# Query projection as three rounded products for 12 of 16 row groups, all query tiles ahead of the cross-attention output, half of its weights loaded behind them

## What is computed

```python
h = rmsnorm(x); q, k, v, u = split(h @ w_in)
x = x + concat([sliding_window_attention(q, k, v), multiscale_pool(u)]) @ w_out
x = x + memory_cross_attention(rmsnorm(x), rmsnorm(mem))   # 4 heads of 128, 256 memory tokens
x = x + hierarchical_moe(rmsnorm(x))                       # 32 experts, top 2 of one group
# memory_cross_attention(h, mem_n):
q = rmsnorm((h @ xq_w).reshape(B, S, 4, 128))              # (512x2048) @ (2048x512)
p = softmax(q . k / sqrt(128)); return (p @ v) @ xo_w      # (512x512) @ (512x2048)
```

## Time and profile before

| | us |
|---|---|
| median of 3 runs | 1630.94 (1630.66 to 1634.11) |
| the profiled execution, its own time | 1631.62 |
| its span in the profile | 1629.7 |
| PE busy | 1517.8 (93%) |
| DVE / ACT / POOL busy | 604.6 / 365.5 / 443.8 |
| HBM read | 466.99 MB, 289 GB/s over the span |

### The profile page before, as it was taken

The page is one execution under the profiler, slowest core; times in us unless marked ns, Lnnn a source line. Parts: engine busy times, 40 slices in busy tenths (PEclk is TensorE's granted clock), DMA queues, the critical chain, the costliest instruction groups (busy, mean ns, idle before and its releaser), DMA issues.

```text
span 1629.7 us, 22070 instructions
## 1 busy us (share of the span) xinstructions
PE 1517.8 (93%) x6992; PEld 848.6 (52%) x6992; DVE 604.6 (37%) x746; ACT 365.5 (22%) x702; POOL 443.8 (27%) x2170
## 2 busy tenths in 40 slices
PE   7999999999999999899899899889999889989998
PEld 7787777758887466633243333323433333333333
DVE  6755656662324433523133223313313313312324
ACT  6422334352222244421011110110011101011011
POOL 4470035420000000044243332422423324233220
PEclk9999999999999999999999999999999999999999
DMA  8332222262324111599999999999999999999997
GB/s 311 104 104 77 78 78 75 84 193 96 103 78 147 59 54 50 233 369 428 427 427 429 427 429 428 429 429 427 429 428 428 430 428 429 428 428 430 428 424 298
DMA packets 88849, 471.93 MB, mean 290 GB/s; under 512 B 4642, under 2 KB 42716, under 8 KB 62556
## 3 DMA queue, kind: packets, MB, share of 16 engines
q1 hardware_dynamic: 88232, 470.84, 71.1%
q0 software_dynamic: 464, 0.35, 0.4%
q10 hardware_dynamic: 100, 0.03, 0.0%
HBM read 466.99 MB, written 4.21 MB: 289 GB/s over the span
## 4 chain that ended last, share of the span: by engine, by line
PE 70%; DMA 18%; DVE 6%; ACT 2%; issue 2%; SPq 1%; POOL 1%; ACTq 0%; DVEq 0%
PE ps L2310 22%; DMA weight_ring<-in_expert_w_up_dram 17%; PE ps L2010 11%; PE ps L1884 10%; PE ps L2340 7%; PE ps L2267 6%; PE ps L2063 3%; DVE residual L1692 2%; PE ps L1846 1%; PE ps L2404 1%; DMA residual<-in_x_dram 1%; PE ps L2126 1%; ACT weight_ring L922 1%; PE ps L1939 1%; PE ps L2123 1%
## 5 line engine op out<-in xcount | busy, mean ns | idle before, releaser
L2310 PE MATMUL ps<-weight_ring,proj_buffer 128*64 128x512 f32 x2040 | 474.3, 605 | 41.0 <-DMA weight_ring<-in_expert_w_up_dram 39.6
L722 POOL COPY proj_buffer<-transposed_acts (+1 forms) x1968 | 300.0, 215 | 616.7 <-ACT proj_buffer L1104 480.1
L2310 PEld LDWEIGHTS ps<-weight_ring,proj_buffer 128*64 128x64 f32 x2040 | 159.1, 139 | 344.5 <-issue 282.3
L1692 DVE TENSOR_TENSOR residual<-ps,residual 128x1024 f32<-128x1024 f32 x128 | 150.8, 1220 | 248.8 <-PE ps L2267 248.2
L2340 PE MATMUL ps<-weight_ring,proj_buffer 128*64 128x512 f32 x944 | 209.2, 595 | 15.6 <-issue 13.6
L1708 DVE SCALAR_TENSOR_TENSOR y_low<-ps,proj_buffer,y_high 64x1024 fp32r<-64x1024 f32 x60 | 77.0, 1283 | 231.4 <-ACT y_high L1115 230.4
L2340 PEld LDWEIGHTS ps<-weight_ring,proj_buffer 128*64 128x64 f32 x944 | 71.2, 137 | 136.1 <-issue 133.6
L1115 ACT ACTIVATE y_high<-ps,proj_buffer 64x1024 fp32r<-64x1024 f32 x60 | 66.5, 1109 | 285.0 <-PE ps L2340 284.3
L1884 PE MATMUL ps<-mix_high,w_in_high 128*128 128x512 f32 x288 | 117.3, 407 | 1.4 <-issue 1.4
L1104 ACT ACTIVATE proj_buffer<-ps 128x512 f32<-128x512 f32 x32 | 19.1, 598 | 438.0 <-PE ps L2310 438.0
L1884 PE MATMUL ps<-mix_high,w_in_low 128*128 128x512 f32 x288 | 112.3, 390 | 0.0
(11 more groups left out here) (330 smaller groups left out, 1812.7 us busy)
## 6 DMA issues: line engine op xcount, KB each, us to landing
weight_ring<-in_expert_w_down_dram SPq DMA_DIRECT2D x62, 2048.0 KB, 15.1
weight_ring<-in_expert_w_up_dram SPq DMA_DIRECT2D x61, 2048.0 KB, 20.3
weight_ring<-in_expert_w_gate_dram SPq DMA_DIRECT2D x60, 2048.0 KB, 15.9
weight_ring<-in_w_in_dram SPq DMA_DIRECT2D x18, 1024.0 KB, 5.6
weight_ring<-in_w_out_dram SPq DMA_DIRECT2D x16, 1024.0 KB, 5.0
weight_ring<-in_xkv_w_dram SPq DMA_DIRECT2D x8, 1024.0 KB, 7.5
residual<-in_x_dram SPq DMA_DIRECT2D x8, 1024.0 KB, 12.6
weight_ring<-in_expert_w_gate_dram SPq DMA_DIRECT2D x7, 1024.0 KB, 10.6
```

The costliest lines, as they stand in the source:

```text
L722: ins = g.tensor_copy(slots[:, :, j], H[:, :, ds(where[j], 1)].rearrange("p k n -> p (k n)"))
L1692: v.tensor_tensor(part, ps[:, bank:bank + 2, :].rearrange("p b n -> p (b n)"), part, ALU.add).then_inc(signal, 1)
L2310: ins = mm(ps[side * SLOTS:(side + 1) * SLOTS, 0, :], xsT[:, k, par * SLOTS:(par + 1) * SLOTS], gate_up_weights(e, u, kk), start=(k == 0), ...
```

## The change

`KQ = 12`: the first 12 of the 16 row groups of a query tile are made from rounded parts, three products each, and the last 4 as plain fp32 as before. For that

- ACT makes `xq_hi` (16 scaled copies of 128x512, the gain of the norm now multiplied into the weights) and DVE makes `xq_lo` (12), in between the steps for n = 3; the parts for k = 7 to 11 can only be written after the last output product (`halves_used`);
- the transposed rows are copied out of PSUM by ACT (`query_rows`, 4 copies a tile, no gain) in place of DVE (`turned`), and DVE subtracts (`query_rows_low`, 3 a tile). For tiles 2 and 3 ACT does so after `query_squares(0)`;
- xq_hi takes slots 8 to 11, so xo_w's parts 2 and 3 are loaded only once all queries are done, and `xo_high(2)`, `xo_high(3)`, `xo_low(2)`, `xo_low(3)` move behind `values_high(1)` and `values_out(1)`;
- PE runs `queries(3)` ahead of `cross_out(0)`.

```diff
@@ SP
             sp.wait_ge(halves_used, HALVES_IN + 32)
             for n in range(4):
+                if n == 2:
+                    sp.wait_ge(xq_done, NT)
                 sp.dma_start(xo_raw[n], xo_v[:, :, n * 512:(n + 1) * 512]).then_inc(landed[4 + 2 * n], 16)
             for u in (1, 2, 0, 3, 4, 5):
-                if u == 1:
-                    sp.wait_ge(used, SEQ_XQ + 2)
-                if u == 2:
-                    sp.wait_ge(xq_done, NT)
@@ ACT
-            for t in range(NT):
-                square_of(3, t)
-                root_of(6 + t)
+            def xq_high(first, last):
+                for k in range(first, last):
+                    if k % 4 == 0:
+                        chunk_landed(act, SEQ_XQ + k // 4)
+                    if k == 7:
+                        act.wait_ge(halves_used, HALVES_IN + 32)
+                    raw = chunk(SEQ_XQ + k // 4, XW)[:, k % 4, :]
+                    a.activation(xq_hi[k] if k < KQ else raw, raw, ACT.Copy,
+                                 scale=gT[:, G_XAT + k:G_XAT + k + 1]).then_inc(xq_hi_ready, 1)
+            def query_rows(t):
+                for b in range(4):
+                    act.wait_ge(h_turned, (6 + t) * 4 + b + 1)
+                    dst = (mix_hi if b < 3 else H)[:, 4 * b:4 * b + 4, t * P:(t + 1) * P]
+                    a.activation(dst, ps[:, b, :].rearrange("p (k n) -> p k n", n=P), ACT.Copy).then_inc(hT_ready, 1)
+            square_of(3, 0)
+            root_of(6)
+            xq_high(0, 4)
+            square_of(3, 1)
+            root_of(7)
+            xq_high(4, 7)
+            square_of(3, 2)
+            query_rows(0)
+            root_of(8)
+            xq_high(7, KQ)
+            square_of(3, 3)
+            query_rows(1)
+            root_of(9)
+            xq_high(KQ, KD)
@@ DVE
             add_part(3, 0)
             scale_rows(0)
+            xq_low(0, 4)
             add_part(3, 1)
             scale_rows(1)
+            xq_low(4, 7)
             add_part(3, 2)
-            turned(6, H, 0, G_XAT)
+            query_rows_low(0)
             scale_rows(2)
             add_part(3, 3)
-            turned(7, H, P, G_XAT)
+            xq_low(7, KQ)
+            query_rows_low(1)
             scale_rows(3)
-            turned(8, H, 2 * P, G_XAT)
-            turned(9, H, 3 * P, G_XAT)
+            query_rows_low(2)
+            query_rows_low(3)
@@ PE, turn_scaled
                     pe.wait_ge(hT_ready, T * 4 + (b - 3))
+                    if t > 0 and b < 3:
+                        pe.wait_ge(rows_lo_ready, 3 * t + b - 2)
@@ PE, queries
+                        if k < KQ:
+                            for n, (h_, w_) in enumerate(((mix_hi[:, k, part], xq_hi[k]), (mix_hi[:, k, part], xq_lo[:, k, :]),
+                                                          (rows_lo[t][:, k, :], xq_hi[k]))):
+                                ins = mm(ps[:, 4 + t % 2, :], h_, w_, start=(k == 0 and n == 0), stop=False)
+                        else:
+                            ins = mm(ps[:, 4 + t % 2, :], H[:, k, part], w[:, kk, :], start=False, stop=(k == KD - 1))
@@ PE
             xscores(1)
-            cross_out(0)
+            queries(3)
             xturn(1)
...
             xscores(2)
-            queries(3)
+            cross_out(0)
             xturn(2)
```

76 lines of the change are left out of this document (58 added, 18 removed).

## The result

The changed kernel took **1638.12 us**, median of six runs (1636.91 to 1640.53), beside 1632.34 for the kernel before in six: ratio 1.0035, 95% interval 1.0024 to 1.0046. So it is slower by 0.2 to 0.4%, 3.8 to 5.8 us; the forecast was +3.9. The 16 runs together have a median of 1637.5, and that is the figure the experiments are set against.

What follows compares the result with a forecast made beforehand. PE was taken as the path up to the first expert block, expert weight transfers after it. Terms gave +1.3 without the clock, +2.6 for the clock, +3.9 in all: 1634.8 us from a median of 1630.94, range 1629.5 to 1639.5.

Steps and rivals of the forecast that it cites:

- products: Query tiles on PE: three rounded products replace an fp32 one in 12 row groups, over four tiles -8.5 us.
- tile 3 into the banks: At turn_scaled(3): PE waits for banks that ACT and DVE empty later than before, +1.5 us (0.5 to 2.5).
- xvalues(1): Tile 1's value products: ACT does query_squares(3) before the copy they need; a wait of 2.0 us, +1.3.
- cross_out(0), third quarter: Waits for add_cross(0), behind late weight transfers and xnorm(2) on DVE: +3.7 us; 0 if transfers land early, 5.5 if slowed.
- cross_out(1), third quarter: Waits for its addition because ACT makes the router's rows ahead of xexps(3): +4.2 us (2 to 5).
- turn_queries(3): The old wait for query_scaled(3), now done some 10 us ahead, goes: -1.6 us.
- clock: Falls behind both third-quarter waits, +3.4 us, less 0.8 for the old fall at 637 that might go: +2.6 (0 to 5).
- The new work of ACT and DVE ahead of queries(0): Scaled copies and subtractions for the rounded parts, taken as covered: 0, up to +2 us if either slips.
- The drain: Rival: two table loads on the path each bring a drain, +2.8 us on top, 1637.6 us; chance 0.02.
- a rival, with 1.7: More falls and a late transfer: clock also falls at xvalues(1), +1.7, or PE is held up, +2; 1637 to 1640; 0.12.
- the clock holds: Rival: the clock holds or falls where it costs nothing; +1.3 alone, 1632 to 1633 us, no change; chance 0.27.
- the covered waits: Rival: add_cross is not late at either third quarter, so 7.9 us of waits go: -6.6, 1624.3 us; chance 0.09.

Runs made afterwards that it cites:

- The 16 runs: The changed kernel as it is, in two measurements: six runs, 1638.12 us, and ten runs, 1636.96 us.
- experiment 6: Changed kernel with dummy products on PE inside its three long waits, the waits for other engines left in place: 1633.55 us, ratio 1.0001.
- experiment 4: Kernel before with only the changed kernel's order on PE, ACT and DVE, query products plain, cross weights staged in one go: 1644.05 us, ratio 1.0062.
- experiment 3: Changed kernel with tile 1's probability copy ahead of query tile 3's squares on ACT: 1637.75 us, ratio 1.0029.
- experiment 1: Changed kernel with tile 3's exponentials ahead of token tile 0's root and scaled rows on ACT, DVE's order moved to match: 1628.81 us, ratio 0.9972.
- experiment 2: Changed kernel with the first cross output's additions on DVE taken one by one, ahead of tile 2's probabilities: 1630.99 us, ratio 0.9991.
- experiment 7: Changed kernel with 24 in place of 18 dummy products ahead of the first expert block: 1639.27 us, ratio 1.0036.
- experiment 9: Changed kernel with experiment 1 and experiment 2 together, without the moves of the probability copy and row copies: 1623.71 us, ratio 0.9945.
- the kernel with all mends: Changed kernel with experiment 1, experiment 2, experiment 3 and tile 2's row copies ahead of tile 0's squares on ACT: 1620.95 and 1620.74 us.

## Why the prediction was right, and where its steps were off

The forecast was +3.9 us and 1634.8; measured were +5.8 and +3.8, and 1638.1 and 1637.0, inside the range. Slower by over 0.2% was the likeliest case, and it came, by the waits that the prediction named. That the second difference meets the forecast within 0.1 is luck: the two measurements are 2.0 apart, and the query stage grew by 5.7 where the steps gave 1.3 + 3.4 = 4.7. The times lie 3.3 and 2.2 us over the 1634.8, of which 1.4 and 2.2 are the kernel before, which came out at 1632.3 and 1633.2 in the larger sets and not at 1630.9. By its own steps:

| step | forecast | shown |
|---|---|---|
| products | -8.5 | -8.2 (tile: 13.74 to 11.69) |
| tile 3 into the banks | +1.5 | +1.46 (1.11, then 2.26 for 1.91) |
| xvalues(1) | +1.3 | +1.30 (2.01 for 0.71) |
| xvalues(2) | +0.7 | +0.71 |
| cross_out(0), third quarter | +3.7 | +3.54 where no fall came ahead of it (+3.13 and +2.63 behind one) |
| cross_out(1), third quarter | +4.2 | +4.49 |
| turn_queries(3) | -1.6 | -1.63 |
| sum without the clock | +1.3 | +1.7; the stage of experiment 6, without a fall, is +1.8 |
| clock | +2.6 | +3.9 in the stage; the old fall stayed in one trace, and went (-1.4) in the other |

**The products and the front.** The new work of ACT and DVE ahead of queries(0) was covered: PE has no wait at turn_scaled(1) nor in queries(0), and goes from one to the next as before. Experiment 4 puts products and banks together at 7.0.

**cross_out(0), third quarter**, is right in mechanism and size wherever the clock does not fall ahead of it. I started the chain at the end of queries(3) and let the fourth part of xo_w land 7.73 us after the issue, then one high part, one low part and the softmax chain, 16.5 in all. In experiment 3 the issue stands at

```profile
584.18 0.92 SPq L524 DMA_DIRECT2D weight_ring<-in_xo_w_dram  x2
```

and ACT, which waits for the landing, starts on the fourth part at 591.87 (its rows there), 7.69 us later. In experiment 1 the issue is at 587.02, ACT starts at 594.78, also out of a wait for the landing, and the third quarter at 603.50: 7.76 and 16.48. In the changed kernel itself another path came last: the fall at xvalues(1), which I had not put into the forecast, made `values_high(1)` late, the landings were there when ACT came to them, and both low parts, 3.43 us, stood between the high parts and xmax(2). That the wait is then 3.13, and 2.63 with a shorter fall, the steps do not give. My lower bound of 0 for early landings was wrong: in experiment 4 nothing lands late and the wait is 3.19, since both low parts still stand ahead of xmax(2).

**cross_out(1), third quarter** was right in mechanism and near in size, 4.49 for 4.2. Missing from its sum is the table load ahead of root_of(10) (613.37): from the start of `values_high(2)` to the rows it takes 2.33 us where I had 2.0. The load ahead of root_of(11), which experiment 1 takes away, is no cost of the change. The kernel before has it too (at 634.33, 1.28 us), with the same wait of 1.97 behind it.

**The drain.** The two loads that came onto the path are there, and again without a drain behind them; ahead of root 3:

```profile
584.77 1.28 ACT L1066 ACT_TABLE_LOAD   x1
586.06 0.30 ACT L1066 ACTIVATE query_stats<-query_stats,eps 128x4 f32<-128x4 f32 x1
```

The root starts 0.01 us after the load's end. The drain of about 1.38 us that ScalarE: Activation LUTs of the Trainium skill, section What ACT_TABLE_LOAD costs, adds to a load would have made the waits at xvalues(1) and at cross_out(1) 1.4 longer each; they are within 0.3 of what the load alone gives. That rival is out.

**The clock** is the term that was mis-sized. I took 1.7 for each of the two waits of 4 us; they cost 1.3 and 1.4 in the first trace, so 2.7 for 3.4, though behind 5.11 and 4.49 us of idle time experiments 3 and 2 show 2.2 and 2.5. I took no fall behind the 2.0 us at xvalues(1) into the forecast (it was in a rival, with 1.7); it fell there in both traces of the changed kernel and cost 1.2 net, and held in experiments 1, 2 and 4 behind the same wait. And I booked 0.8 for a fall at 637 that might go; it stayed in the first trace and went in the second. Experiment 6 settles the size: 3.4 us by the medians and 3.9 in the stage hang on the three waits, where the forecast had 2.6 for the clock in all.

**The rivals.** That the clock holds fell to the windows, the covered waits to the waits themselves; experiments 1 and 2 show what would have made the latter true, and it is the order, not the transfers.

## What to carry to other kernels

When a step is moved ahead on one engine, write out what each other engine has queued ahead of the work that the next step waits for; here 8 us saved on PE were lost because two additions of 0.7 us stood behind softmax chains of 5 to 12 us, and moving a few steps won 17. Put functions of the same table together: one step moved on ScalarE took two loads of 1.28 us off the path. Price a wait of PE together with the clock fall that can follow it: behind waits of 2.0 to 5.1 us in this stage the falls cost 1.2 to 2.5 us each, and behind those of 2.0 they came in some executions and not in others. Dummy products in the wait bought the falls back without touching the wait.

## What the runs showed that I had not expected

- Behind the same wait of 2.0 us at xvalues(1) the 16 products took 3.62 and 3.13 us in the two traces of the changed kernel, 2.95 in experiment 7 and 2.78 in experiment 9, and 2.05 in experiments 1, 2 and 4. No row ahead of it that I read differs between the changed kernel and experiments 1 and 2; what decides it stays open.
- A faster stretch can end slower: 18 dummies at the full clock took 4.23 us, left 2.75 us of idle time, and block 0 began with 8.78 us; at a lower clock they took 5.4, left 1.4, and it began with 7.09. The two kinds reached the end of that half 15.8 and 13.9 us after the dummies' start.
- With the long waits gone the times lie closer together: 1619.9 to 1622.4 us in the nine runs of the kernel with all mends, 1634.3 to 1640.8 in the 16 of the changed one. Falls that come in some executions and not in others would do this, but it is not shown: the kernel before has none of the long waits, and its times lie as far apart, 1630.0 to 1635.4 in 22 runs.
